# High and low gate weights in one stationary block of 128 columns, in the opening of a hybrid mLSTM and attention layer

## The reference

```python
h = rms_norm(x, g_norm[l]) * (1.0 + scale) + shift
proj = h @ w_in[l]
xa, va, oa, za, ia, fa, qa, ka, vat, zb, ga, gb = jnp.split(proj, split_at, axis=-1)
xc = jax.nn.silu(causal_depthwise_conv(xa, w_conv[l], b_conv[l]))
q_m = jnp.einsum('bshd,hde->bshe', xc_h, w_q_mlstm[l])
k_m = jnp.einsum('bshd,hde->bshe', xc_h, w_k_mlstm[l]) * (MLSTM_HEAD_DIM ** -0.5)
h_m = mlstm_chunkwise(q_m, k_m, v_m, ia + b_igate[l], fa + b_fgate[l])
```

## Time and profile before

| | us |
|---|---|
| median of 3 runs (1430.76 to 1431.08) | 1431.03 |
| profiled execution | 1430.43 |
| its span in the trace | 1428.6 |
| TensorE busy | 1408.3 (99%) |
| VectorE busy | 817.4 (57%) |
| ScalarE busy | 508.8 (36%) |
| GpSimd busy | 382.0 (27%) |

### The profile page before, as it was taken

The page is one execution under the profiler, slowest core; times in us unless marked ns, Lnnn a source line. Parts: engine busy times, 40 slices in busy tenths (PEclk is TensorE's granted clock), DMA queues, the critical chain, the costliest instruction groups (busy, mean ns, idle before and its releaser), DMA issues.

```text
span 1428.6 us, 17210 instructions
## 1 busy us (share of the span) xinstructions
PE 1408.3 (99%) x6701; PEld 1176.7 (82%) x6701; DVE 817.4 (57%) x1367; ACT 508.8 (36%) x922; POOL 382.0 (27%) x209
## 2 busy tenths in 40 slices
PE   8999999999999999999999999999999999999996
PEld 6788888888888888888888888888887888888885
DVE  7876557366466745545474544547599326433565
ACT  7645223532323353132235323233453346111122
POOL 3032111222211122221111221112138873222541
PEclk9999999999999999999999999999999999999998
DMA  8321111043111115210111421011151306332443
GB/s 301 139 74 49 45 31 31 30 153 105 63 57 45 45 38 163 74 45 30 31 30 31 149 74 45 30 31 30 32 162 30 133 1 235 105 124 94 147 147 103
DMA packets 51818, 117.19 MB, mean 82 GB/s; under 512 B 20753, under 2 KB 20881, under 8 KB 51734
## 3 DMA queue, kind: packets, MB, share of 16 engines
q1 hardware_dynamic: 47786, 103.49, 22.2%
q10 hardware_dynamic: 2832, 8.53, 1.9%
q0 software_dynamic: 1120, 4.06, 1.0%
HBM read 100.64 MB, written 15.43 MB: 81 GB/s over the span
## 4 chain that ended last, share of the span: by engine, by line
PE 90%; DVE 3%; DMA 3%; ACT 2%; POOL 1%; issue 1%; SPq 0%; DVEq 0%; ACTq 0%; POOLq 0%
PE banks L532 25%; PE banks L534 25%; PE banks L533 25%; PE banks L829 2%; PE banks L819 2%; DMA x_rows<-in_x 2%; PE banks L780 2%; PE banks L786 2%; DVE y L2075 1%; PE banks L838 1%; PE banks L766 1%; PE banks L778 1%; POOL wlo L1577 1%; PE banks L497 1%; PE banks L523 1%; PE banks L498 1%
## 5 line engine op out<-in xcount | busy, mean ns | idle before, releaser
L672 POOL TENSOR_TENSOR wlo<-wraw,whi 128x1024 fp32r<-128x1024 f32 x77 | 196.9, 2558 | 849.5 <-ACT whi L916 832.8
L532 PE MATMUL banks<-h_hi,whi 128*128 128x512 f32 x1000 | 399.7, 400 | 1.6 <-POOL wlo L1577 1.3
L534 PE MATMUL banks<-h_hi,wlo 128*128 128x512 f32 x1000 | 390.5, 391 | 0.0
L533 PE MATMUL banks<-h_lo,whi 128*128 128x512 f32 x1000 | 389.5, 390 | 0.0
L534 PEld LDWEIGHTS banks<-h_hi,wlo 128*128 128x128 f32 x1000 | 187.7, 188 | 40.0
L532 PEld LDWEIGHTS banks<-h_hi,whi 128*128 128x128 f32 x1000 | 188.0, 188 | 39.5 <-issue 3.3
L533 PEld LDWEIGHTS banks<-h_lo,whi 128*128 128x128 f32 x1000 | 188.1, 188 | 36.6
L916 ACT ACTIVATE whi<-wraw 128x1024 fp32r<-128x1024 f32 x75 | 78.9, 1053 | 85.8 <-PE banks L534 73.6
L532 PE MATMUL banks<-whi,h_hi 128*128 128x512 f32 x240 | 93.5, 390 | 0.0
L534 PE MATMUL banks<-whi,h_lo 128*128 128x512 f32 x240 | 93.4, 389 | 0.0
L533 PE MATMUL banks<-wlo,h_hi 128*128 128x512 f32 x240 | 93.4, 389 | 0.0
(11 more groups left out here) (377 smaller groups left out, 2592.9 us busy)
## 6 DMA issues: line engine op xcount, KB each, us to landing
wraw<-in_w_all SPq DMA_DIRECT2D x92, 512.0 KB, 3.6
s_wada<-in_w_ada_cols SPq DMA_DIRECT2D x16, 512.0 KB, 5.7
raw_lo<-in_x SPq DMA_DIRECT2D x8, 512.0 KB, 9.7
qm<-group_weights SPq DMA_DIRECT2D x8, 512.0 KB, 6.4
mlstm_branch<-xc SPq DMA_DIRECT2D x8, 512.0 KB, 9.0
part<-in_w_ada_gate SPq DMA_DIRECT2D x16, 256.0 KB, 3.6
sig_c<-in_w_all SPq DMA_DIRECT2D x8, 512.0 KB, 4.3
um_lo_raw<-mlstm_branch SPq DMA_DIRECT2D x8, 512.0 KB, 4.9
```

The source lines that it names most:

```text
L532: t_.matmul(out, w_hi, x_hi, start=first, stop=False)
L533: t_.matmul(out, w_hi, x_lo, start=False, stop=False)
L534: return t_.matmul(out, w_lo, x_hi, start=False, stop=last)
L672: nc.gpsimd.tensor_tensor(wlo[:, hi, :], wraw[:, q % 2, :], whi[:, hi, :].bitcast(F32), ALU.subtract).then_inc(w_split, 1)
```

## The change

The gates' high and low weights lie side by side in one block of 128 columns: high in columns 0 to 63, low in 64 to 127. One matmul multiplies both with `h_hi`, one more multiplies both with `h_lo` (which adds the product of the two low parts, left out before). A step k has 10 matmuls on `h_hi` and 6 on `h_lo`. The sums come in four groups of rows of banks 4 and 5: rows 0 to 3 and 64 to 67 for the input gates, 32 to 35 and 96 to 99 for the forget gates. ScalarE copies the four out, with the bias on the high ones, straight after the matmuls. VectorE no longer reads PSUM; it waits for all four rows, adds them by pairs and takes the minimum with 0, before the convolution. The absolute value, which ScalarE took while reading, becomes an operation of its own ahead of the exponential.

```diff
-    ("s_gw_raw", [P, KT, 64], F32), ("s_gw_hi", [P, KT, 64], F32R), ("s_gw_lo", [P, KT, 64], F32R),
+    ("s_gw_raw", [P, KT, 64], F32), ("s_gw", [P, KT, P], F32R),
...
+    gw_hi, gw_lo = gw[:, :, 0:64], gw[:, :, 64:]
...
-                     (gw_hi[:, k, :], gw_lo[:, k, :], ps[0:64, 4:6, :]))
+                     (gw[:, k, :], None, ps[:, 4:6, :]))
...
-                t_.matmul(to[:, h, :], w_lo, hi, start=False, stop=False)
+                if w_lo is not None:
+                    t_.matmul(to[:, h, :], w_lo, hi, start=False, stop=False)
...
-                        pe.wait_ge(gate_parts, 2)
+                        pe.wait_ge(gate_parts, 4)
...
             def gate_rows():
 
+                act.wait_ge(g_ready, 2)
+                act.wait_ge(small_in, 64)
+                A(rows[:, 3, :], ps[32:32 + HEADS, 4:6, :], ACT.Identity, bias=gb[32:32 + HEADS, 1:2]).then_inc(gate_parts, 1)
+                A(rows[:, 2, :], ps[96:96 + HEADS, 4:6, :], ACT.Copy).then_inc(gate_parts, 1)
+                A(rows[:, 0, :], ps[0:HEADS, 4:6, :], ACT.Identity, bias=gb[0:HEADS, 0:1]).then_inc(gate_parts, 1)
+                A(rows[:, 1, :], ps[64:64 + HEADS, 4:6, :], ACT.Copy).then_inc(gate_parts, 1)
+
+            def gate_logs():
                 act.wait_ge(gate_read, 1)
-                act.wait_ge(small_in, 64)
-                A(rows[:, 2, :], ps[32:32 + HEADS, 4:6, :], ACT.Abs, bias=gb[32:32 + HEADS, 1:2]).then_inc(gate_parts, 1)
-                A(rows[:, 0, :], ps[0:HEADS, 4:6, :], ACT.Identity, bias=gb[0:HEADS, 0:1]).then_inc(gate_parts, 1)
-
-            def gate_logs():
-                act.wait_ge(gate_parts, 2)
+                A(rows[:, 2, :], rows[:, 5, :], ACT.Abs).then_inc(gate_parts, 1)
+                act.wait_ge(gate_parts, 5)
                 A(rows[:, 2, :], rows[:, 2, :], ACT.Exp, scale=-1.0).then_inc(gate_parts, 1)
...
         dve.wait_ge(g_ready, 2)
-        v.tensor_scalar(row(3), ps[32:32 + HEADS, 4:6, :], gb[32:32 + HEADS, 1:2], 0.0, ALU.add, ALU.min).then_inc(gate_read, 1)
         v.memset(v1[:, :, DH:DH + 2], 1.0).then_inc(ready, 1)
...
         dve.wait_ge(ready, 2)
+        dve.wait_ge(gate_parts, 4)
+        v.tensor_tensor(row(5), row(3), row(2), ALU.add).then_inc(gate_read, 1)
+        T["shared"]["step"](v.tensor_tensor(row(0), row(0), row(1), ALU.add))
+        dve.wait_ge(gate_read, 1)
+        T["shared"]["step"](v.tensor_scalar(row(3), row(5), 0.0, None, ALU.min))
```

More of the change, by code:

```diff
@@ L272, in setup @@
     small_in, pos_in, g_ready, x2_split = (T[n] for n in ("small_in", "pos_in", "g_ready", "x2_split"))
-    wada, gw_raw, gw_hi, gw_lo, gn, bc, ms, xs, _, x2_hi, x2_lo, xnT, crow, sq = T["setting"].values()
+    wada, gw_raw, gw, gn, bc, ms, xs, _, x2_hi, x2_lo, xnT, crow, sq = T["setting"].values()
+    gw_hi, gw_lo = gw[:, :, 0:64], gw[:, :, 64:]
     c_in, gw_in = sem("c_in"), sem("gw_in")
@@ L333, in gpsimd @@
         pool.wait_ge(gw_split, 1)
-        nc.gpsimd.tensor_tensor(gw_lo[:], gw_raw[:], gw_hi[:].bitcast(F32), ALU.subtract).then_inc(gw_split, 1)
+        nc.gpsimd.tensor_tensor(gw_lo, gw_raw[:], gw_hi.bitcast(F32), ALU.subtract).then_inc(gw_split, 1)
     def scalar(act):
@@ L376, in scalar @@
         act.wait_ge(gw_in, 16)
-        A(gw_hi[:], gw_raw[:], ACT.Copy).then_inc(gw_split, 1)
+        A(gw_hi, gw_raw[:], ACT.Copy).then_inc(gw_split, 1)
         act.wait_ge(c_silu, 4)
@@ L927, in gate_rows @@
             def gate_rows():
-                act.wait_ge(gate_read, 1)
-                act.wait_ge(small_in, 64)
-                A(rows[:, 2, :], ps[32:32 + HEADS, 4:6, :], ACT.Abs, bias=gb[32:32 + HEADS, 1:2]).then_inc(gate_parts, 1)
-                A(rows[:, 0, :], ps[0:HEADS, 4:6, :], ACT.Identity, bias=gb[0:HEADS, 0:1]).then_inc(gate_parts, 1)
-            def gate_logs():
-                act.wait_ge(gate_parts, 2)
+                act.wait_ge(g_ready, 2)
[5 more added lines that the diff above has]
+            def gate_logs():
+                act.wait_ge(gate_read, 1)
+                A(rows[:, 2, :], rows[:, 5, :], ACT.Abs).then_inc(gate_parts, 1)
+                act.wait_ge(gate_parts, 5)
                 A(rows[:, 2, :], rows[:, 2, :], ACT.Exp, scale=-1.0).then_inc(gate_parts, 1)
-                act.wait_ge(gate_parts, 3)
+                act.wait_ge(gate_parts, 6)
                 A(rows[:, 2, :], rows[:, 2, :], ACT.Ln, bias=1.0).then_inc(gate_parts, 1)
@@ L1105, in vector @@
         dve.wait_ge(ready, 2)
+        dve.wait_ge(gate_parts, 4)
[3 more added lines that the diff above has]
+        T["shared"]["step"](v.tensor_scalar(row(3), row(5), 0.0, None, ALU.min))
         def gate_sums():
-            dve.wait_ge(gate_read, 1)
-            dve.wait_ge(gate_parts, 4)
+            dve.wait_ge(gate_parts, 7)
             dve.wait_ge(consts, 7)
```

## The result

The changed kernel takes 1434.64 us, median of nine runs (1432.28 to 1435.85); the kernel before takes 1431.03 on the same chips (nine runs, 1430.20 to 1431.82). The ratio is 1.0024 with a 95% interval from 1.0016 to 1.0033: 3.6 us slower. 16 matmuls are gone and the kernel has lost time.

A forecast was written before the change was run, and what follows sets the result against it. The prediction took TensorE to bound the kernel (90% of the chain), with VectorE's h_lo close behind in the opening. Opening -1.50, later tile +4.40 and clock +1.3 made +4.2 us: 1435.2 on the median, range 1432.2 to 1437.3.

The forecast's parts named there:

- The opening: Eight steps before the token tiles: VectorE's h_lo pace limits the gain from 16 removed matmuls to 1.50 us, not 3.69.
- The reads: ScalarE's four gate-row reads delay its keep of the second projection, costing TensorE 0 to 0.3 us at the third token tile.
- The tile 2.9 us later than now: Fourth tile of TensorE's next token block: waits for fold_low, ending 81.88; 2.9 us later, replacing the opening's gain.
- case C: Small stall, because minimum and tensor_scalar aren't held on GpSimd's turns: +1.5 us, 1432.5; chance 0.10.
- The clock: TensorE's idle 3.5 us before fold_low lowers its clock; 1.3 us taken as half of a possible 2.4.
- case A: Stall at fold_low and the clock falls: 1435.2, own range 1434.0 to 1436.9; chance 0.52.
- Further on: After the tile, up to the keep of q's first half at 120.44: no further loss, 0 us, bound 1.5.
- The sum: Whole kernel: -1.50 + 4.40 + 1.3 = +4.2 us, giving 1435.2 on the median.
- B: Same stall at fold_low, but the clock stays at 1.00: 1433.9; chance 0.20.
- F: A second wait, for gate rows or the first keep behind the rotary tables: 3 us more, 1438; chance 0.07.

The follow-up runs named there:

- block alone: Kernel before with the 128-column block and two matmuls for three, gates' rows read as before, low weights' sums left out: 1429.09 us.
- two scratch rows: Changed kernel with adds moved behind, high forget row read by VectorE, and two alternating scratch rows for VectorE's modulation products: 1427.12 us.
- short wlo: Changed kernel with the head loop's first two wlo cut from 1024 to 128 columns on GpSimd: 1428.69 us.
- reads alone: Changed kernel with the third matmul put back, 18 matmuls a step, new reads and adds kept: 1435.58 us.
- stall filled: Changed kernel with 12 matmuls adding zero in TensorE's stall ahead of the fourth tile of its second token block: 1432.96 us.
- first four runs: The first group of follow-up kernels; the kernel before, measured again beside them in 29 executions, took 1430.90 us.
- adds behind: Changed kernel with VectorE's two adds and minimum moved from ahead of head 0's convolution to behind its output's low parts: 1428.86 us.
- one row read by VectorE: Changed kernel with the adds moved behind and the high forget row read from PSUM by VectorE, the other three by ScalarE: 1429.48 us.
- minimum behind: Changed kernel with only the minimum moved behind, into the cumulative sums, the two adds staying ahead of the convolution: 1433.92 us.

## Why the prediction was right

- *The opening, "gain 1.50 us".* Measured 1.56, and 1.55 with the block alone. The recurrence (h_lo's end, 0.05, then 1.48 for six matmuls) holds to the hundredth: 57.17 + 1.22 + 0.05 = 58.44, and step 7 at 59.93. Shown from both sides: less work for TensorE doesn't come through in full (block alone), less for VectorE does (two scratch rows). The 0.06 us more is TensorE's pace: the 16 matmuls of step 7, where it doesn't wait, take 63.56 - 59.93 = 3.63 us and not 3.69. That shows too that the wider block costs TensorE nothing; the opening's length alone wouldn't, since VectorE's pace would hide it.
- *The reads, "0 to 0.3 us".* 0.34, in the changed kernel covered by the later wait, uncovered where the adds are moved.
- *"The tile 2.9 us later than now".* The opening's 1.56 against 4.25: 2.69 at the tile's first matmul, where the forecast had 81.93 - 79.14 = 2.79, and 0.10 more for the restart, which the low clock hides. On the way the wait for the second wlo was 0.48 us, not 0.9, and the stall itself 3.0, not 3.5; neither moves the tile, since fold_low's end sets it. fold_low was forecast 19.59 us behind the opening's end (81.88 - 62.29) and came 19.54. Turn for turn, the minimum and the tensor_scalar were held, as worked out from the one row at 15.13; case C is excluded by that, and by the run with short wlo.
- *The clock, "1.3 us".* The step whose size was least supported: the 6.4 us at the lower clock that it halves stand in no row of a stall, and half of the 2.4 is 1.2. It fell, as in case A. It cost 1.7 us in the changed kernel's profile and 2.9 in that of the reads alone, and filling the stall gained 1.7 by the medians. That 1.3 lies so near is luck. It isn't the same in each execution. The changed kernel's nine lie 3.6 us apart, and their mean granted clocks, which are on record for each, go with the times: 0.997 at 1432.28 and 1434.44, 0.996 or 0.995 in the seven others, 0.995 in three of the four slowest. (3.4 us at half rate are 1.7 us of full clock, 0.0012 of the span.) With the stall filled, seven of eleven have 0.997 or 0.998 and take up to 1433.13, four have 0.996 and take 1433.77 and more. The kernel before has low ones as well: of the 29 beside the first four runs the nine slowest, from 1431.96 on, have 0.996 or 0.995, and that the prediction didn't foresee. A mean doesn't tell where in the kernel the clock fell, and one execution with the stall filled (1436.36 at 0.996) and one with the adds behind (1433.04 at 0.996) are slower than a single fall explains.
- *Further on, "I count 0".* Right for the head loop: behind the low clock TensorE keeps one distance from the kernel before up to 1103. Not foreseen was the merging stage. There TensorE waits for GpSimd's wlo, 0.9 us up to 1103.4 in the kernel before, and what was gained is partly given back: 1.56 to 1.05 and then 0.77 with the block alone, 1.16 to 0.76 with the adds behind; with one row read by VectorE it grew instead, from 1.62 to 1.86. Why it differs from one execution to the next stays open.
- *The sum.* 1435.2 was forecast, 1434.64 measured: +4.2 against +3.6. In the profiled execution -1.56, +4.25 and +1.66 make +4.35, and with the 1.33 of the setting-up TensorE is 5.68 us behind from the tile on. The merging stage adds 0.5, and behind the last matmul the kernel before takes 0.75 longer (11.83 against 11.08): 5.4, the difference of the spans. This execution had two falls of the clock; what they cost can be less in others, and the medians lie 3.6 us apart. The chances have a slip: A, half of B and F are 0.69, not 0.67.

The Trainium skill ("TensorE: Matmul & The Clock Gate", Part 1), by which activity has to release the throttle again, agrees with these traces: after the stall TensorE worked without a gap, and the rate of 0.50 still lasted from 83.5 to 86.7. The Trainium skill ("SBUF — State Buffer", SBUF: two separate sides) calls the pair of ports that VectorE and GpSimd share an exclusive lock, held for a whole instruction; that agrees with the minimum's 2.78 us for 0.68 in the changed kernel.

## What to carry to other kernels

Before counting removed matmuls as time, compare the pace of the engine that feeds them: with 4.147 us a step for TensorE and 3.975 for VectorE, only 0.17 us a step could be won, and 0.23 us taken off VectorE was then worth as much as 16 matmuls. When small work goes to the front of an engine's queue, add not its own length but what the queue behind it will now run into; 0.7 us of minimum on four partitions met a 2.3 us turn of GpSimd, and so did the instruction behind it. Put such work where its engine waits anyway, and if a stall of TensorE of some 3 us can't be avoided, filling it with idle matmuls can pay, 1.7 us here.

## What the runs showed of the hardware

- VectorE and GpSimd, with work from SBUF to SBUF queued on both, took turns instruction by instruction behind the opening, and a one-input operation of VectorE on four partitions was held as long as one on 128 (2.78 us for 0.68, 2.77 for 0.81, in the changed kernel). Shortening GpSimd's instructions from 1024 to 128 columns freed VectorE (0.84 each).
- TensorE's granted clock fell to 0.50 around the end of an idle time of 3.0 us (changed), 3.1 (reads alone) and also of 2.3 (minimum behind, where TensorE was idle from 78.7 to 81.0 and the clock was at 0.50 from 81.0 to 84.3), and in the setting-up once behind 2.1 us, where 1.5 to 1.9 us in six profiles and 2.6 to 2.8 us in three (15.6 to 18.4 with the adds behind, for one) left it at 1.00. So the length of the idle time alone doesn't tell whether it falls.
- With twelve matmuls on zero weights in the idle time, the clock stayed at 1.00 in the profiled execution.
- VectorE and ScalarE read one PSUM bank at once without loss, on different rows of it (32 to 35 against 96 to 99 and 0 to 3): 1.27 and 1.02 us, and the keep came 1.1 us earlier. The same rows at once weren't tried.
